# Layer 1's conditioning products move from the prompt attention into the state-space scan of a two-layer decoder step

## The reference

```python
for layer in range(2):
    mp = ada_modulation(c_prompt, ada_w[layer], ada_b[layer])    # silu(c) @ w + b, w: 1024 x 6144
    ms = ada_modulation(c_sample, ada_w[layer], ada_b[layer])
    h = modulate(rmsnorm(x, ln_mix_g[layer]), m[0], m[1])
    # layer 0: even_mixer: SSD scan (16 heads x 64, state 128) and stick-breaking attention
    # layer 1: odd_mixer: gated short convolution
    x = x + m[2] * mixer(h)
    x = x + m[5] * hier_moe(modulate(rmsnorm(x, ln_ffn_g[layer]), m[3], m[4]))
y = rmsnorm(x, final_g)
```

## Time and profile before

| what | before |
|---|---|
| median of 3 runs | 1782.37 us (1776.14 to 1785.35) |
| the profiled execution | 1777.82 us |
| its span | 1776.1 us |
| PE busy | 1472.2 us, 83% |
| DVE busy | 652.4 us, 37% |
| ACT busy | 460.8 us, 26% |
| POOL busy | 190.6 us, 11% |
| mean granted clock of PE | 0.895 |

### The profile page before, as it was taken

The page is one execution under the profiler, slowest core; times in us unless marked ns, Lnnn a source line. Parts: engine busy times, 40 slices in busy tenths (PEclk is TensorE's granted clock), DMA queues, the critical chain, the costliest instruction groups (busy, mean ns, idle before and its releaser), DMA issues. The chain is left out here.

```text
span 1776.1 us, 25336 instructions
## 1 busy us (share of the span) xinstructions
PE 1472.2 (83%) x10279; PEld 1086.0 (61%) x10279; DVE 652.4 (37%) x1268; ACT 460.8 (26%) x804; POOL 190.6 (11%) x314
## 2 busy tenths in 40 slices
PE   4999789868989677699479978858999849988875
PEld 1999544455679433499345544548999825554435
DVE  3322266543245575652621111143246451111114
ACT  3212265532124442331301100032224221110012
POOL 0000033310000142100011111020000001111002
PEclk8999899988989787699779999968999869999995
DMA  7222497649921601411889999941223298999974
GB/s 292 72 88 79 187 361 263 238 169 338 372 77 48 245 1 43 159 48 48 329 330 390 378 392 398 395 154 48 72 96 98 82 409 320 388 390 395 391 267 151
DMA packets 133593, 399.73 MB, mean 225 GB/s; under 512 B 15842, under 2 KB 67682, under 8 KB 110690
## 3 DMA queue, kind: packets, MB, share of 16 engines
q1 hardware_dynamic: 114370, 359.01, 53.9%
q10 hardware_dynamic: 11488, 21.24, 3.3%
q0 software_dynamic: 7616, 17.84, 3.2%
HBM read 368.72 MB, written 37.19 MB: 229 GB/s over the span
## 5 line engine op out<-in xcount | busy, mean ns | idle before, releaser
L2871 PE MATMUL ex_gups<-ex_gu,ex_he 128*64 128x256 f32 x1728 | 211.8, 401 | 46.4 <-DMA ex_gu<-in_moe_w_up 43.5
L2871 PEld LDWEIGHTS ex_gups<-ex_gu,ex_he 128*64 128x64 f32 x1728 | 127.0, 144 | 115.2 <-DMA ex_gu<-in_moe_w_up 48.3
L2916 DVE TENSOR_TENSOR ex_hid<-ex_sg,ex_gups 128x128 f32<-128x128 f32 x64 | 18.4, 288 | 299.8 <-ACT ex_sg L2940 299.8
L2889 PE MATMUL ex_yps<-ex_dn,ex_hid_t 128*64 128x512 f32 x512 | 123.9, 604 | 0.9 <-issue 0.9
L2849 POOL DMA_INDIRECT ex_hg<-h_rows,route_tok x64 | 60.2, 941 | 510.0 <-PE ex_trps L2861 425.6
L225 PE MATMUL sc_ps<-h_hi,sc_hi 128*128 128x272 f32 x352 | 101.7, 289 | 0.5 <-PEq L3115 0.5
L225 PE MATMUL sc_ps<-hT_r,sc_hi 128*128 128x272 f32 x352 | 100.9, 287 | 0.0
L225 PE MATMUL sc_ps<-h_hi,sc_w_r 128*128 128x272 f32 x352 | 100.7, 286 | 0.0
L2940 ACT ACTIVATE ex_sg<-ex_gups 128x128 f32<-128x128 f32 x64 | 17.7, 277 | 300.1 <-PE ex_gups L2871 300.1
L2930 ACT ACTIVATE ex_yo<-ex_yps 128x512 f32<-128x512 f32 x64 | 38.2, 597 | 184.9 <-PE ex_yps L2889 184.9
L2909 DVE COPY ex_he<-ex_trps 128x512 f32<-128x512 f32 x64 | 44.3, 692 | 63.9 <-PE ex_trps L2861 63.9
(11 more groups left out here) (535 smaller groups left out, 3397.9 us busy)
## 6 DMA issues: line engine op xcount, KB each, us to landing
ex_dn<-in_moe_w_down SPq DMA_DIRECT2D x64, 1024.0 KB, 26.5
ex_gu<-in_moe_w_gate SPq DMA_DIRECT2D x54, 1024.0 KB, 25.4
ex_gu<-in_moe_w_up SPq DMA_DIRECT2D x54, 1024.0 KB, 26.7
ada_rest_w<-in_ada_w SPq DMA_DIRECT2D x40, 1024.0 KB, 6.5
as_pages<-in_cache_kT SPq DMA_DIRECT2D x32, 512.0 KB, 6.5
as_pages<-in_cache_v SPq DMA_DIRECT2D x32, 512.0 KB, 5.6
y_rows<-ex_yo ACTq DMA_DIRECT2D x128, 128.0 KB, 7.0
qkv_w<-in_mix_w_in SPq DMA_DIRECT2D x12, 1024.0 KB, 5.4
```

The source lines that it names most:

```text
L2871: last = nc.tensor.matmul(gu_ps[64 * q:64 * q + 64, :, :], he[n % 2][:, j, :], ex.gu[n % S][:, :, j, q * P:(q + 1) * P], start=(j == 0), s ...
L2889: last = nc.tensor.matmul(y_ps[n % 2][64 * c:64 * c + 64, :], hid_t[:, m * CAP:(m + 1) * CAP], ex.dn[n % S][:, m, c * 512:(c + 1) * 512], ...
L2916: nc.vector.tensor_tensor(hid[:, :], sg[:, :], gu_ps[:, 1, :], ALU.mult).then_inc(done["hid"], 1)
```

## The change

- The prompt attention keeps only the two parts of layer 0. Their tiles are spread over 15 steps each instead of six.
- Layer 1's 6144 columns become six parts of 1024 columns (tiles of 512 KB, four matmuls of 256 columns, two slots) in the scan. Two tiles each stand at 24 of the half steps ("points") from step 2 on: at an even point behind the decay sums, at an odd one at the end of the step. ACT copies the sums, PE turns them, DVE stores them, and the two scales of layer 1 are folded at step 17.
- To make room, `sst` becomes a ring of six states. States 6 and 7 are loaded into the places of 0 and 1 when these have been stored. The last round of sample sums moves from step 10 to step 14, the preparation of chunk 3 one step earlier. The matmuls of C with B go into the bank of the transposes, so that the conditioning has a bank.
- The first weight of the output projection is loaded at step 17 of the scan; the last three stores of states are waited for in the output projection. There ACT splits the weight's upper half after the second square instead of after the eighth.
- In both combines POOL adds the eight squared tiles down to two, and PE makes two matmuls instead of eight.

```diff
+    def __init__(self, k, name, parts, slots, ctx, at=None, cols=2048, rows_at=None):
+        self.k, self.parts, self.slots, self.COLS = k, parts, slots, cols
+        if rows_at is not None:
+            self.w = k.sb(f"{name}_w", [P, slots, self.COLS], ctx=ctx)
+            self.rows = k.nc.alloc_sbuf_tensor_at(f"{name}_rows", [P, cols // 4], F32, offset=rows_at)
...
+        n = self.COLS // 4
         for g in range(4):
             last = nc.tensor.matmul(sum_ps[32 * g:32 * g + 32, :], self.k.cT[:, j, :],
-                                    self.w[:, (part * KT + j) % self.slots, g * 512:(g + 1) * 512], start=(j == 0),
+                                    self.w[:, (part * KT + j) % self.slots, g * n:(g + 1) * n], start=(j == 0),
                                     stop=(j == KT - 1), skip_group_check=True)
...
-    AT = (0, 0, 1, 2, 2, 3, 4, 4)
-    SPAN = 6
+    AT = (0, 2, 4, 5, 7, 9, 10, 12)
+    SPAN = 15
-    copy_at, turn_at, store_at = ({SPAN * part + d: part for part in range(len(ada.parts))} for d in (5, 5, 6))
+    copy_at, turn_at, store_at = ({SPAN * part + d: part for part in range(len(ada.parts))} for d in (13, 13, 14))
...
-                ada.fold(dve, [(0, 4, "ln_ffn"), (1, 1, "ln_mix"), (1, 4, "ln_ffn")])
+                ada.fold(dve, [(0, 4, "ln_ffn")])
...
+class OutAhead:
+
+    KEPT = 3
+
+    def __init__(self, k, w, at):
+        self.k, self.w = k, w.rearrange("(k p) n -> p k n", p=P)
+        self.at, self.raw = at, k.nc.alloc_sbuf_tensor_at("out_ahead", [P, 2 * KT, 256], F32, offset=at)
+        self.w_half, self.late = k.sem("oa_w_half"), k.sem("oa_late")
+
+    def load(self, sp):
+        sp.dma_start(self.raw[:, KT:2 * KT, :], self.w[:, KT:2 * KT, 0:256]).then_inc(self.w_half, 16)
+        sp.dma_start(self.raw[:, 0:KT, :], self.w[:, 0:KT, 0:256]).then_inc(self.k.w_ready[0], 16)
...
-               4: [(2, 0)], 5: [(2, 1), (4, 0)], 6: [(2, 2), (4, 1)], 7: [(2, 3), (4, 2), (4, 3)],
-               9: [(3, 0)], 10: [(3, 1)], 11: [(3, 2)], 12: [(3, 3)]}
-    SUMS_AT, TURN_SUMS_AT = {9: (0, 1), 10: (2, 3)}, {11: (0, 1), 12: (2, 3)}
+               4: [(2, 0)], 5: [(2, 1), (4, 0)], 6: [(4, 1), (2, 2)], 7: [(2, 3), (4, 2), (4, 3)],
+               8: [(3, 0)], 9: [(3, 1)], 10: [(3, 2)], 11: [(3, 3)]}
+    SUMS_AT, TURN_SUMS_AT = {9: (0, 1), 10: (2,), 14: (3,)}, {11: (0, 1), 12: (2,), 16: (3,)}
     FIRST_UPDATE = 11
+    RING = 6
+    LATE_PARTS, LATE_SPAN, LATE_FROM = 6, 5, 4
+    late_products, late_turn, late_copy = {}, {}, {}
+    for part in range(LATE_PARTS):
+        base = LATE_FROM + LATE_SPAN * part
+        for j in range(KT):
+            late_products.setdefault(base + j // 2, []).append((part, j))
+        late_copy[base + 3], late_turn[base + 4] = part, part
     DECAY_AT = {10: (0, 1), 11: (2,), 12: (3,), 13: (4,), 14: (5,), 15: (6,), 16: (7,)}
...
-        sst = k.sb("sst", [P, NB, D], ctx=ctx)
-        ac_ps = k.ps("ss_acps", [P, 512], ctx)
+        sst_ring = k.sb("sst", [P, RING, D], ctx=ctx)
+        ada = AdaWeights(k, "ada_late", [(1, part) for part in range(LATE_PARTS)], 2, ctx, cols=1024,
+                         rows_at=k.offset["neg_ones"])
+        ac_ps = y_ps[1]
+        ada_bank = k.ps("ss_ada", [P, 512], ctx)
+        ada_ps = ada_bank[:, 0:256]
...
-                sp.dma_start(sst[:, :, :], io["ssm_state"]).then_inc(s["sload"], 16)
+                def load_states(t):
+                    one = (2 * t) % RING
+                    sp.dma_start(sst_ring[:, one:one + 2, :], io["ssm_state"][:, 2 * t:2 * t + 2, :]).then_inc(s["sload"], 16)
+
+                for m in range(ada.slots):
+                    ada.load(sp, 0, m)
+                for t in range(RING // 2):
+                    load_states(t)
                 sp.wait_ge(s["zeroed"], 1)
                 for i in range(NE * CAP, NBLK * CAP, P):
                     sp.dma_start(k.y_rows[i:i + P, :].rearrange("p (c f) -> p c f", c=4),
                                  zeros[:, :].unsqueeze(1).to_broadcast([P, 4, 256])).then_inc(s["stored"], 16)
-                for g in range(2):
-                    sp.wait_ge(emptied[g], bank_no["chunk", 3] + 1)
-                sp.dma_start(io["ssm_p"], st[:, 1, :]).then_inc(s["stored"], 16)
-                for b in range(NB):
+
+                def load_late(m):
+                    sp.wait_ge(ada.used, m - ada.slots + 1)
+                    ada.load(sp, m // KT, m % KT)
+
+                def store_state(b):
                     for g in range(2):
-                        sp.wait_ge(emptied[g], bank_no["update", b] + 1)
-                    sp.dma_start(io["ssm_s"][:, b, :], sst[:, b, :]).then_inc(s["stored"], 16)
-                sp.wait_ge(s["stored"], 16 * (1 + NB + OVB * CAP // P))
+                        sp.wait_ge(emptied[g], bank_no["update", b, g] + 1)
+                    done = out_ahead.late if b >= NB - out_ahead.KEPT else s["first_out"] if b < 2 else s["stored"]
+                    sp.dma_start(io["ssm_s"][:, b, :], state(b)).then_inc(done, 16)
+
+                def store_prompt_state():
+                    for g in range(2):
+                        sp.wait_ge(emptied[g], bank_no["chunk", 3, g] + 1)
+                    sp.dma_start(io["ssm_p"], st[:, 1, :]).then_inc(s["stored"], 16)
+
+                point_of = {part * KT + j: point for point, some in late_products.items() for part, j in some}
+                for point in range(2 * (FIRST_UPDATE + NB)):
+                    for m in range(ada.slots, LATE_PARTS * KT):
+                        if point_of[m - ada.slots] == point:
+                            load_late(m)
+                    step = point // 2
+                    if point % 2 == 0:
+                        if step == 17:
+                            sp.wait_ge(s["y"], N)
+                            out_ahead.load(sp)
+                        continue
+                    if step == POS[3, 1]:
+                        store_prompt_state()
+                    if step >= FIRST_UPDATE:
+                        store_state(step - FIRST_UPDATE)
+                    if step == FIRST_UPDATE + 1:
+                        sp.wait_ge(s["first_out"], 32)
+                        load_states(3)
+                sp.wait_ge(s["stored"], 16 * (1 + NB - 2 - out_ahead.KEPT + OVB * CAP // P))
...
+                    if pairs_before[c, part]:
+                        pe.wait_ge(s["cbc"], pairs_before[c, part])
                     g0, g1 = GROUPS[part]
...
-                    last.then_inc(s["tr"], 1)
                     if part == 2:
+                        for g in range(2):
+                            last = nc.tensor.matmul(tr_ps[0:n, 256 + g * P:256 + g * P + n], xc[:, 8 + g, a:a + n],
+                                                    xc[:, 10 + g, a:a + n], start=True, stop=True)
                         if c == 0:
                             pe.wait_ge(s["aexp"], 5)
-                        else:
-                            pe.wait_ge(s["cbc"], cb_no[c])
-                        for g in range(2):
-                            last = nc.tensor.matmul(ac_ps[0:n, 256 + g * P:256 + g * P + n], xc[:, 8 + g, a:a + n],
-                                                    xc[:, 10 + g, a:a + n], start=True, stop=True)
-                        last.then_inc(s["cb"], 1)
+                    last.then_inc(s["tr"], 1)
...
+                def condition(point):
+                    for part, j in late_products.get(point, ()):
+                        m = part * KT + j
+                        if j == 0 and part:
+                            pe.wait_ge(ada.out, part)
+                        pe.wait_ge(ada.ready[m % ada.slots], 16 * (m // ada.slots + 1))
+                        ada.products(ada_ps, part, j)
+                    if point in late_turn:
+                        pe.wait_ge(ada.copied, late_turn[point] + 1)
+                        ada.turn(ada_ps)
 
                 for part in range(3):
                     turn(0, part)
                 for i in range(FIRST_UPDATE + NB):
                     if i < N:
                         decay_sums(i)
+                    condition(2 * i)
...
+                def keep_condition(point):
+                    if point in late_turn:
+                        dve.wait_ge(ada.turned, late_turn[point] + 1)
+                        ada.store(ada_ps, late_turn[point])
...
-                    if i == 12:
+                    if i == 16:
                         sample_result()
                     if i >= FIRST_UPDATE:
                         update(i - FIRST_UPDATE)
+                    keep_condition(2 * i + 1)
+                    if i == 17:
+                        dve.wait_ge(ada.out, LATE_PARTS)
+                        ada.fold(dve, [(1, 1, "ln_mix"), (1, 4, "ln_ffn")])
...
+                def copy_rows(point):
+                    if point in late_copy:
+                        act.wait_ge(ada.used, KT * (late_copy[point] + 1))
```

(26 more changed lines are left out.)

110 lines of the change are left out of this document (63 added, 47 removed).

## The result

The changed kernel takes 1807.7 us, median of four runs (1807.35 to 1810.72), against 1783.4 for the kernel before on the same chip: a ratio of 1.0152, 95% interval 1.0126 to 1.0178. The forecast was 1778, the range 1759 to 1797. It is slower by 24 us, outside the range. Its profiled execution has a span of 1806.3 us, 30.2 more than before's.

The account below looks back on a forecast made before the run. The kernel was taken as a row of stages that nothing overlaps. Terms: attention -24.4, scan +34.4, exit -2.4 and -3.3, squares -5.0 and -3.7, sum -4.4 us; from 1782.4 to 1778.0, range 1759 to 1797.

Parts of the forecast that it names:

- Attention: Prompt attention: 24 of 40 conditioning tiles leave, shortening the start by 9 us and later steps by 15.5; -24.4 us.
- Rival (c): Prompt attention: its ACT and DVE chain holds more steps, -12 instead of -24.4; net +8, 1790 us; chance 0.09.
- Scan, steps 2 to 7: Early scan: a chain of late weight loads through two slots appears and holds the steps; +18.4 us.
- 4.3 us per pair: Scan: one turn of the load chain, from 3.5 landing, 0.48 product and some 0.3 issue and second load.
- Scan, steps 8 to 18: Later scan: 14 pairs of products, waits for their loads and SP's wait for stores; +16 us.
- The mean half step is 3.9 us against 4.3 for a pair: 14 x 0.4: Scan, steps 8 to 18: waiting for loads, reckoned from the mean half step; 5.6 us.
- the pairs right behind the decay sums are hidden: Scan, steps 8 to 18: these pairs run while ACT and DVE make the weighted matrix, so they cost nothing.
- SP's wait for the stores of states 0 and 1: Scan, step 12: SP waits before loading states 6 and 7, delaying step 13's loads; 0.4 us.
- Exit: Scan's end and output projection: later waits for stores -2.4 us, earlier statistics -3.3 us.
- Squares: Both combines: fewer PE matmuls after POOL adds; -5.0 us in the last, -3.7 in layer 0's, set by DVE's weight split.
- (a): Scan: the products fill idle PE stretches at a higher clock, steps 8 to 18 at +1; net -19.4, 1763 us; chance 0.28.
- (b): Scan: load waits drop the granted clock to 0.5 in steps 2 to 7; net +14, 1796 us; chance 0.15.

Follow-up runs that it names:

- products_only: scan_form plus all late products, copies, turns and stores in the scan, but only the first two tiles loaded; 1783.0 us, 1.0012 of the kernel before.
- scan_form: The changed kernel with all five conditioning parts back in the prompt attention and none in the scan; 1765.4 us, 0.9917 of the kernel before.
- zeros_late: The changed kernel with the eight zero stores issued one by one at the ends of steps 8 to 15; 1808.5 us, 1.0127 of the kernel before.
- loads_only: scan_form plus all 48 late loads, waited for by PE, with one small matmul per tile instead of the products; 1825.2 us, 1.0240 of the kernel before.

## Why the prediction was wrong

**Attention: right in the main.** -24.4 was forecast, -20.1 measured up to the scan's start; the attention stage itself is 17.9 us shorter and ends at 361.4, not near 354. A round is 17.7 us (17 to 18 forecast); the first four steps take 19.4 us (18.6 forecast), 8.3 us less; the next 27 steps give 11.8 us (15.5 forecast). Among them is a first step of a round that a tile mostly at PE's lower level stretched (1.77 us for the tile at a granted clock of 0.57; 5.4 us from 256.18 to 261.56). Of seven profiles with five parts, before's has the shortest way from the attention's start to the scan; against the other six the gain on this way is 21 to 28 us. Rival (c), -12, didn't happen.

**Scan, steps 2 to 7: the mechanism right, its size wrong.** +18.4 forecast, +31.1 measured. The term that failed is "4.3 us per pair". It took a load's best time of 3.5 us for the landing and 0.3 for the second load. Late loads took at least 3.7 in the changed kernel (4.3 in the median), the second tile comes at least 1.2 us behind the first, and SP issues it only when its own product is done. The second pair, whose loads stood behind the zero stores:

```profile
603.86 1.08 PE L542 MATMUL ss_ada<-ada_late_w,cT_sb 128*32 128x256 f32 x8 [5.45 <-DMA ada_late_w<-in_ada_w]
605.09 1.08 PE L542 MATMUL ss_ada<-ada_late_w,cT_sb 128*32 128x256 f32 x8 [0.15 <-DMA ada_late_w<-in_ada_w]
```

Its products end at 606.17, 12.0 us behind the start of step 2 (594.13); the sum had 623.1 - 614.21 = 8.9, so 3.1 us of the miss are here. From there to step 8 it took 654.14 - 606.17 = 48.0 us, 6.0 for each of the eight further pairs, where the sum had 34.4 + 4 = 38.4: another 9.6 us. The two are the 12.7 us that were missed.

**Scan, steps 8 to 18: the step that failed.** +16 forecast, of them 5.6 for waits; with the stores +13.6, measured +30.6. Two sentences were wrong. "The mean half step is 3.9 us against 4.3 for a pair: 14 x 0.4": points aren't evenly spaced. Between an odd and the next even point lie only the decay sums, 2 us, and a long half step doesn't pay for a short one, because with two slots no load can be issued ahead. The sum of the waits is the sum over each distance, not one over their mean. And "the pairs right behind the decay sums are hidden": PE waited there as well. Its waits for late weights from step 8 on are 18.4 us, where I had 5.6: 8.7 behind the decay sums and 9.7 at the ends of steps. Summed over distances, 46.5 - 22.2 = 24.3 us lie in these steps (at 5.4 us a pair); at the forecast's own 4.3 us a pair it is still 15. By these estimates the mean accounts for some 10 us and the price for some 9. The products, 10 us in my sum for this stretch, were right where no load is waited for: 8.1 in products_only (91.8 us from step 8 on against 83.7 in scan_form).

A term too small was SP's wait for the stores of states 0 and 1, 0.4 us in the sum. In the changed kernel, step 13 (its first pair is used from 714.29 on):

```profile
711.14 0.38 SPq L1603 DMA_DIRECT2D out_ssm_s<-sst  x1
716.36 0.33 SPq L1584 DMA_DIRECT2D sst<-in_ssm_state  x1
716.74 8.44 SPq L532 DMA_DIRECT2D ada_late_w<-in_ada_w  x4
...
722.47 1.08 PE L542 MATMUL ss_ada<-ada_late_w,cT_sb 128*32 128x256 f32 x8 [3.65 <-DMA ada_late_w<-in_ada_w]
```

The next tile is there 8.2 us after the pair's use begins, where it is 4.8 in step 12 (702.17 to 706.97), and PE waits 3.65 us for it, its longest wait from step 8 on. So this wait, with the states' 1 MB that is loaded right behind it, costs some 3 us, once (an estimate from these rows).

**Exit: right.** -2.4 for the stores (the stage ends 0.9 us behind the last update, where it was 3.0: 2.2), -3.3 for the statistics, measured 3.2. **Squares: right in the last combine,** -5.3 (5.0 forecast), **near in layer 0's,** -2.8 (3.7), where the split of the weight was to set the statistics. The split took as long as before, but the statistics are read 3.0 us behind its end. POOL's add that ran beside it took 2.94 us, where the same add took 1.26 to 1.53 us the other seven times:

```profile
1230.44 1.26 POOL L3248 TENSOR_TENSOR co_sq<-co_sq 128x512 f32<-128x512 f32 x1 [1.46 <-ACT co_sq L3312]
...
1233.07 2.29 DVE L3343 TENSOR_TENSOR sc_w_r<-sc_w,sc_hi 128x2048 fp32r<-128x2048 f32 x1
1233.54 2.94 POOL L3248 TENSOR_TENSOR co_sq<-co_sq 128x512 f32<-128x512 f32 x1 [1.02 <-ACT co_sq L3312]
```

In this one place the two engines got in each other's way, as the prediction had it, but POOL was the one held up, and its add is on the way to the statistics: 1.7 us, an estimate from these rows, more than the 0.9 that are missing.

**Rivals.** (a), the scan absorbs the products: it doesn't, even without their loads. It had steps 8 to 18 at +1 us; in products_only they are 8.1 us longer, and the scan 17.1. (b), the clock: 0.86 in steps 2 to 7, above the 0.7 from which it would have decided, and 0.81 behind, above the 0.78 of before; with the products and no loads it is 0.88 there (products_only). It is lower in zeros_late (0.76 over the scan) and in loads_only (0.71), where PE waits and has no products. Slower was in my cases, as (b), at 1796 us, but by the clock and not by the waits; the measured time lies beyond it.

**The sum with measured terms**: -20.1 (up to the scan) + 61.8 (scan, stores in it) - 3.2 - 2.8 - 5.3 = +30.4; the spans differ by 30.2.

## What to carry to other kernels

Before work that needs loads is moved beside other work, list the distances between the places where it is consumed, and sum max(0, refill time - distance), where the refill time runs from a slot's last use to the landing of the last load of the batch; with only as many slots as one place consumes, a long gap pays nothing back. The sum gives the size, not where the waits will stand. Twice the slots took a lengthening of 31.4 us down to 6.2 for the same loads. And ask for the marginal price in the place the work leaves: here the fifth part of the conditioning cost 7 to 12 us and the third 2 to 5, so moving three parts was not worth it. Moving one was no loss, but starting the tiles one step later gained as much without moving any.

## What the runs showed of the hardware

- Two loads of 512 KB issued one behind the other landed 4.2 and 5.4 us after their slots were used; the second comes 1.2 us behind the first (loads_only). Of 256 KB the quickest landed in 2.6 us, of 512 KB in 3.6 to 3.7.
- PE's granted clock fell in the stage whose waits had little work between them: 0.71 in loads_only, 0.83 in scan_form, with some 20 us more busy time for the same matmuls. The 17.1 us of products then cost only 6.6 on top of the loads.
- A 128x512 add on POOL took 2.94 us beside a 128x2048 subtraction on DVE and 1.26 to 1.53 us otherwise; the subtraction took 2.29 us with and without it.
- The same attention with five parts took 179.6 to 187.2 us in seven profiles of kernels that don't differ there. So a single stage's length in one profile is uncertain by some 2% either way.
